# Recurrence of a bidirectional RWKV-7 layer: merged products on TensorE, one sum on GpSimd, wider state copies

## The reference, cut to what matters

```python
def _rwkv7_step(S, inp):
    r, w, k, v, a, b = inp
    Sa = jnp.einsum('zbhvk,zbhk->zbhv', S, a)
    S = S * w[..., None, :] + Sa[..., :, None] * b[..., None, :] + v[..., :, None] * k[..., None, :]
    return S, jnp.einsum('zbhvk,zbhk->zbhv', S, r)
_, ys = lax.scan(_rwkv7_step, S0, xs)          # 256 steps, two directions
y = jnp.moveaxis(ys[:, 0] + jnp.flip(ys[:, 1], axis=0), 0, 1)
```

## Time and profile before

| what | value |
|---|---|
| median of three executions | 1836.3 us |
| the profiled execution | 1839.07 us, its span 1837.1 us |
| TensorE busy in the span | 1708.0 us (93%) |
| VectorE busy | 586.1 us (32%) |
| ScalarE busy | 353.8 us (19%) |
| GpSimd busy | 64.0 us (3%) |
| recurrence (grams of pair 0 to last outputs of pair 7) | 377.6 to 613.4 us |

### The profile page before, as it was taken

One profiled execution on the slowest core, in us unless ns is written; L12 is line 12 of the kernel. 1 busy time (PEld: TensorE's weight loads), 2 busy tenths in 40 slices (PEclk: granted clock), 3 DMA queues, 4 the chain that ended last, 5 costly groups with the idle time before them and its releaser, 6 DMA issues.

```text
span 1837.1 us, 37200 instructions
## 1 busy us (share of the span) xinstructions
PE 1708.0 (93%) x16166; PEld 1090.9 (59%) x16166; DVE 586.1 (32%) x1300; ACT 353.8 (19%) x945; POOL 64.0 (3%) x96
## 2 busy tenths in 40 slices
PE   5999999988889899999899999999999999999897
PEld 5887888867777544675555455454544454444443
DVE  2000333478886301012222322313132222222233
ACT  2122222156675201123100000000000000000002
POOL 1000000000000000002000000000000000000000
PEclk9999999999999999999899999999999999999999
DMA  9932335200000753527799999999999999999993
GB/s 274 237 110 92 118 113 180 100 3 4 4 4 4 275 184 128 177 92 288 279 424 432 426 430 429 434 426 432 431 428 432 430 429 429 433 428 431 429 421 146
DMA packets 95825, 503.64 MB, mean 274 GB/s; under 512 B 37852, under 2 KB 42352, under 8 KB 76896
## 3 DMA queue, kind: packets, MB, share of 16 engines
q1 hardware_dynamic: 90824, 488.17, 66.4%
q0 software_dynamic: 4640, 13.10, 2.4%
q10 hardware_dynamic: 248, 0.65, 0.1%
HBM read 511.29 MB, written 4.23 MB: 281 GB/s over the span
## 4 chain that ended last, share of the span: by engine, by line
PE 71%; DMA 20%; DVE 6%; issue 2%; ACT 1%; SPq 0%; DVEq 0%; POOLq 0%; ACTq 0%
PE ps L1518 14%; DMA ring<-in_wd 9%; PE ps L2027 9%; DMA rest<-in_wu 8%; PE ps L2149 8%; PE ps L2016 8%; PE ps L1843 6%; PE ps L2035 4%; DMA ring<-in_wu 2%; PE ps L1861 2%; PE ps L1912 2%; PE ps L1929 2%; PE ps L1870 2%; PE ps L2007 1%; PE ps L1732 1%
## 5 line engine op out<-in xcount | busy, mean ns | idle before, releaser
L1518 PE MATMUL ps<-wide,ring 128*128 128x256 f32 x1248 | 275.3, 379 | 3.1 <-ACT wide L539 1.9
L1518 PEld LDWEIGHTS ps<-wide,ring 128*128 128x128 f32 x1248 | 239.0, 195 | 41.8 <-issue 10.1
L1397 DVE TENSOR_TENSOR tokA<-tokA,ps 128x512 f32<-128x512 f32 x256 | 158.4, 680 | 100.3 <-PE ps L2035 100.3
L2027 PE MATMUL ps<-ring,wide 128*64 128x256 f32 x1512 | 169.5, 382 | 17.1 <-DMA ring<-in_wu 17.1
L2149 PE MATMUL ps<-ring,gg 128*64 128x512 f32 x768 | 175.4, 598 | 2.7 <-DMA ring<-in_wd 2.1
L2016 PE MATMUL ps<-ring,wide 128*64 128x256 f32 x1536 | 173.2, 383 | 2.4 <-DVE wide L1385 1.7
L1410 DVE SCALAR_TENSOR_TENSOR gg<-ps,tmp,gg 128x256 f32<-128x256 f32 x32 | 15.5, 484 | 477.6 <-PE ps L2027 477.6
L2027 PEld LDWEIGHTS ps<-ring,wide 128*64 128x64 f32 x1512 | 109.6, 138 | 74.7 <-DMA ring<-in_wu 22.1
L2016 PEld LDWEIGHTS ps<-ring,wide 128*64 128x64 f32 x1536 | 110.0, 138 | 56.7 <-issue 3.3
L2035 PE MATMUL ps<-wide,gg 64*128 64x512 f32 x512 | 135.3, 627 | 0.9 <-ACT wide L815 0.8
L2149 PEld LDWEIGHTS ps<-ring,gg 128*64 128x64 f32 x768 | 50.9, 136 | 121.1 <-issue 111.1
(11 more groups left out here) (365 smaller groups left out, 2047.8 us busy)
## 6 DMA issues: line engine op xcount, KB each, us to landing
ring<-in_wg SPq DMA_DIRECT2D x23, 4096.0 KB, 28.4
ring<-in_wu SPq DMA_DIRECT2D x23, 4096.0 KB, 31.3
ring<-in_wd SPq DMA_DIRECT2D x22, 4096.0 KB, 32.1
rest<-in_wd SPq DMA_DIRECT2D x8, 4096.0 KB, 30.4
ring<-in_w_in SPq DMA_DIRECT2D x7, 4096.0 KB, 15.3
rest<-in_wu SPq DMA_DIRECT2D x7, 4096.0 KB, 30.6
rest<-in_wg SPq DMA_DIRECT2D x7, 4096.0 KB, 29.7
ring<-in_w_out SPq DMA_DIRECT2D x4, 4096.0 KB, 17.1
```

What stands on the lines that cost most here:

```text
L1397: V.tensor_tensor(fin_part(t, h, n), fin_part(t, h, n), ps[:, banks[q][h], :], ALU.add).then_inc(S["added"], 1)
L1518: ins = mm(ps[0:rows_, m % 2, 0:T], lhs, hnT[:, k, :], start=k == 0, stop=k == KD - 1)
L2027: ins = mm(ps[CAP * h:CAP * h + CAP, 1, 0:T], xT[:, k, CAP * i:CAP * i + CAP], w[:, T * h:T * h + T], start=k == 0, stop=k == KD - 1)
```

## The change

Four edits, all inside one pair of the recurrence.

First, in step 5 the two products of chunk c with the same weights (one against GB, one against NB) become one product with 128 moving columns, read as two blocks of 64 (`two_blocks`), whose result goes to two blocks of one PSUM bank. For each g there are then two products of 64 columns and two of 128. The readout correction now lies in columns 0 to 63 and the transition in 128 to 191, and VectorE reads them there.

Second, in step 6 GpSimd first adds the key grams of both directions, two instructions for each pair (tile KS), and TensorE multiplies the values with the sum: 12 products for each b in place of 16. They wait for a new semaphore rw_ks.

Third, in `inputs` both heads are taken at once: weights of 64 rows by 128 columns, 128 moving columns, two products for each (i, z) in place of four. The result is 128 by 128, of which the two diagonal 64x64 blocks are used. Tile SS is widened to take it.

Fourth, ScalarE copies 128 columns of the state (line 687) in place of 64.

Together that is 8 + 8 + 12 = 28 products fewer for each pair.

```diff
--- before.py
+++ after.py
@@ -185,7 +185,8 @@
         KT = late[:, 1536:2048].rearrange("p (z t) -> p z t", z=2)
         BKh = late[:, 2048:3072].rearrange("p (m z t) -> p m z t", m=2, z=2)
         NB = late[:, 3072:4608].rearrange("p (g n) -> p g n", g=4)
-        SS = late[:, 5120:5376].rearrange("p (z i n) -> p z i n", z=2, i=2)
+        KS = late[:, 5632:5888].rearrange("p (b e n) -> p b e n", b=2, e=2)
+        SS = late[:, 5120:5632].rearrange("p (z i n) -> p z i n", z=2, i=2)
         RH = late[:, 7680:8192].rearrange("p (g t) -> p g t", g=4)
         nrm_ = tmp[:, 0:5 * T].rearrange("p (i t) -> p i t", t=T)
         Yp, DEV, VAR, DSQ, BNS = (nrm_[:, i] for i in range(5))
@@ -262,7 +263,7 @@
         sq_done var_done std_done rw_nrm rw_vare rw_std hn_done hn_tr hn_ev_a hn_ev_v tile_mm tile_ev tile_sh lora_act
         lora_mm lora_ev v_tr v_ev rel_mm rel_ok sc_mm sc_sum sc_max pr_done pt_tr pt_ev o_mm ya_done ya_sq ya_hn
         ya_tr ya_ev rw_sq rw_n2 rw_bonus_in rw_bon rw_q rw_exp rw_prep rw_n2e rw_y0e rw_gram rw_mask rw_gnow rw_v0 rw_sums rw_pv rw_kv rw_x0
-        rw_x0ev rw_pt rw_pte rw_rh rw_tte rw_r1 rw_xf rw_xe rw_y0 rw_s rw_se rw_ys rw_yp
+        rw_x0ev rw_pt rw_pte rw_rh rw_tte rw_r1 rw_xf rw_xe rw_ks rw_y0 rw_s rw_se rw_ys rw_yp
         rw_mu rw_dsq rw_var rw_out op_mm op_add xk_mm xk_ev xs_mm xs_max xs_exp xs_p xs_tr xs_trev xo_mm xo_ev
         xw_mm xw_add r_wr r_rows r_tr r_ev r_evv r_mm r_m r_pos r_posok r_oh r_ohv r_tab r_tabok r_cnt r_cntv
         m_gate m_sil m_up m_hg m_tr m_xe m_htr m_hT m_dn m_ya m_yv r_oht r_ohtok r_vals r_pick fin_a comb added w_part gate_rest fin_o pool_step""".split()
@@ -462,6 +463,9 @@
             for n in range(4 * CT):
                 pool.wait_ge(S["rw_mask"], n + 1)
                 pool.tensor_tensor(PRN[1][:, n % 4, :, 1, :], GB[:, n % 4, :, 0, :], eye, ALU.add).then_inc(S["rw_r1"], 1)
+                if n % 4 == 3:
+                    for b in range(TB):
+                        pool.tensor_tensor(KS[:, b], GK[:, b, :, 1, :], GK[:, 2 + b, :, 1, :], ALU.add).then_inc(S["rw_ks"], 1)
             pool.wait_ge(S["rw_tte"], 4 * CT)
             pool.dma_start(tokA[:], a["x"].rearrange("(b p) d -> p b d", p=P)).then_inc(S["x2_in"], 16)
             pool.dma_start(memtok, a["mem"].rearrange("(b p) d -> p b d", p=P)).then_inc(S["mem_in"], 16)
@@ -684,7 +688,7 @@
                 for i in range(3):
                     for z in range(2):
                         act.wait_ge(S["rw_s"], 6 * p + 2 * i + z + 1)
-                        A(SS[:, z, i % 2, :], ps[:, S_BANK[i % 2] + 2 * z, T:T + CH], ACT.Copy).then_inc(S["rw_se"], 1)
+                        A(SS[:, z, i % 2, :], ps[:, S_BANK[i % 2] + 2 * z, T:T + P], ACT.Copy).then_inc(S["rw_se"], 1)
                 if next_:
                     for n in range(3, 8):
                         exponential(p + 2, n)
@@ -1135,10 +1139,10 @@
                     if g == 3 and not last:
                         bonus(p + 1, ps[:, 5, T:2 * T])
                     rh = RH[:, g, :].rearrange("p (c t) -> p c t", c=2)
-                    dc.add(V.tensor_tensor(rh, rh, ps[:, 2 * g:2 * g + 2, P:P + CH], ALU.add))
+                    dc.add(V.tensor_tensor(rh, rh, ps[:, 2 * g:2 * g + 2, 0:CH], ALU.add))
                     c = 1 - b
                     V.scalar_tensor_tensor(TT[:, g, :], cst[:, IC:IC + CH], gam_now[:, 4 * z + 1 + b:4 * z + 2 + b],
-                                           ps[:, 2 * g + c, 0:CH], ALU.mult, ALU.add).then_inc(S["rw_tte"], 1)
+                                           ps[:, 2 * g + c, P:P + CH], ALU.mult, ALU.add).then_inc(S["rw_tte"], 1)
                 if not last:
                     dve.wait_ge(S["rw_tte"], 4 * p + 4)
                     V.tensor_copy(gam_now, gam).then_inc(S["rw_gnow"], 1)
@@ -1680,6 +1684,10 @@
                 def value(q, b, e):
                     return Vtok[q, b, P * p + CH * e:P * p + CH * e + CH]
 
+                def two_blocks(x, y):
+                    assert x.ap[0] == y.ap[0] and y.offset > x.offset
+                    return bass.AP(tensor=x.tensor, offset=x.offset, ap=[x.ap[0], [y.offset - x.offset, 2], [1, CH]])
+
                 def tiles():
                     return [(e, r, half_of(r), half_of(r ^ e)) for e in range(2) for r in range(2)]
 
@@ -1747,14 +1755,15 @@
                 for g in range(4):
                     c = 1 - g % 2
                     pe.wait_ge(S["rw_xe"], 4 * p + g + 1)
-                    for h in range(2):
+                    for h in (1 - c, c):
                         q = half_of(h)
                         for e in range(2):
-                            mm(ps[half_of(e), 2 * g + h, P:P + CH], X[q, g, 1, e, :], GB[q, g, e, 1, :], start=True, stop=True)
-                    q = half_of(c)
-                    for e in range(2):
-                        ins = mm(ps[half_of(e), 2 * g + c, 0:CH], X[q, g, 1, e, :], NB[q, g, P + CH * e:P + CH * e + CH],
-                                 start=True, stop=True)
+                            if h != c:
+                                mm(ps[half_of(e), 2 * g + h, 0:CH], X[q, g, 1, e, :], GB[q, g, e, 1, :], start=True, stop=True)
+                            else:
+                                both = ps[half_of(e), 2 * g + h, 0:T].rearrange("p (k n) -> p k n", k=2)[:, :, 0:CH]
+                                ins = mm(both, X[q, g, 1, e, :], two_blocks(GB[q, g, e, 1, :], NB[q, g, P + CH * e:P + CH * e + CH]),
+                                         start=True, stop=True)
                     if g == 2 and not last:
                         pe.wait_ge(S["rw_bonus_in"], p + 2)
                         ins = mm(ps[:, 5, T:2 * T], ones2, ew[:, BON], start=True, stop=True)
@@ -1767,10 +1776,11 @@
                             q = half_of(h)
                             for e in range(2):
                                 mm(ps[half_of(e), 2 * b + h, T:T + CH], X[q, g, 0, e, :], GB[q, g, e, 1, :], start=z == 0, stop=False)
-                        for h in range(2):
-                            q = half_of(h)
-                            for e in range(2):
-                                ins = mm(ps[half_of(e), 2 * b + h, T:T + CH], value(q, b, e), GK[q, g, e, 1, :], start=False, stop=z == 1)
+                    pe.wait_ge(S["rw_ks"], 2 * p + b + 1)
+                    for h in range(2):
+                        q = half_of(h)
+                        for e in range(2):
+                            ins = mm(ps[half_of(e), 2 * b + h, T:T + CH], value(q, b, e), KS[q, b, e, :], start=False, stop=True)
                     ins.then_inc(S["rw_y0"], 1)
                 pe.wait_ge(S["rw_tte"], 4 * p + 4)
 
@@ -1782,12 +1792,9 @@
                     for z in range(2):
                         c, g, h = chunk(i, z)
                         q = half_of(h)
-                        for e in range(2):
-                            mm(ps[half_of(e), S_BANK[i % 2] + 2 * z, T:T + CH], NB[q, g, P + CH * e:P + CH * e + CH], X[q, g, 0, e, :],
-                               start=True, stop=False)
-                        for e in range(2):
-                            ins = mm(ps[half_of(e), S_BANK[i % 2] + 2 * z, T:T + CH], NB[q, g, T + CH * e:T + CH * e + CH], value(q, g % 2, e),
-                                     start=False, stop=i == 0)
+                        heads = ps[:, S_BANK[i % 2] + 2 * z, T:T + P]
+                        mm(heads, NB[q, g, P:T], X[q, g, 0].rearrange("p e n -> p (e n)"), start=True, stop=False)
+                        ins = mm(heads, NB[q, g, T:T + P], Vtok[q, g % 2, P * p:P * p + P], start=False, stop=i == 0)
                         if i == 0:
                             ins.then_inc(S["rw_s"], 1)
                     if i:
@@ -1797,14 +1804,15 @@
                     c, g, h = chunk(i, z)
                     for e in range(2):
                         q = half_of(e)
-                        ins = mm(ps[q, S_BANK[i % 2] + 2 * z, T:T + CH], TT[q, g, :], SS[q, z, (i - 1) % 2, :], start=False, stop=True)
+                        n = slice(CH * e, CH * e + CH)
+                        ins = mm(ps[q, S_BANK[i % 2] + 2 * z, T + CH * e:T + CH * e + CH], TT[q, g, :], SS[q, z, (i - 1) % 2, n], start=False, stop=True)
                     ins.then_inc(S["rw_s"], 1)
 
                 def outputs(i, z):
                     c, g, h = chunk(i + 1, z)
                     for e in range(2):
                         q = half_of(e)
-                        ins = mm(ps[q, 5 + 2 * z, T + CH * c:T + CH * c + CH], SS[q, z, i % 2, :], RH[q, g, CH * h:CH * h + CH],
+                        ins = mm(ps[q, 5 + 2 * z, T + CH * c:T + CH * c + CH], SS[q, z, i % 2, CH * e:CH * e + CH], RH[q, g, CH * h:CH * h + CH],
                                  start=True, stop=True)
                     ins.then_inc(S["rw_ys"], 1)
```

## The result

The changed kernel takes 1861.99 us (median of four executions, 1861.01 to 1863.51) against 1837.01 (1834.95 to 1843.52) for the kernel before: a ratio of 1.0132, interval 1.0119 to 1.0145. The forecast was 1839.5 with a range of 1833.5 to 1844: the sign is right, the size is not. The profiled execution has a span of 1859.2 us, 22.1 more than the 1837.1 of before; the medians are 25.0 apart.

What follows compares the result with a forecast made beforehand. TensorE bounds middle pairs from the states to turn 7, VectorE from there to the fourth transition. 7 x 0.64 = 4.5 us more, less 0.1, 0.6 and 0.6, gives +3.2: 1836.3 + 3.2 = 1839.5 us, range 1833.5 to 1844.

Steps and rivals of the forecast that it cites:

- the last of the sum: Behind the recurrence: everything waits for rw_yp of the last pair, so the recurrence's +3.2 us passes on whole.
- The block rate is the path: Rival, whole recurrence: instruction supply bounds it, so fewer instructions give 7 us, 1829; with a per-matmul overhead variant, chance 0.14.
- GpSimd slows VectorE: Rival, y0's key-gram additions: they delay VectorE 0.3 us a pair where no reserve is, 1841.6 us; chance 0.12.
- the reserve: VectorE's waits at L1065 in the recurrence, taken as 1.7 us for each pair, enough to absorb GpSimd's additions.
- GpSimd loses, not VectorE: Beside the added key-gram sums: GpSimd's operation slows from 0.41 to 0.52 us beside a VectorE copy; cost taken as 0.
- Row halves do not overlap: Rival, state inputs: each inputs call costs 0.44 us more, two on the path, 7 us in all, 1846.5; chance 0.1.
- the tail is covered: Rival, end of each pair: tile changes, loads and copies hide, a pair loses 0.2 us, not 0.64; 1836.5, chance 0.14.
- inputs(1): State-input products of both heads, on the path in each pair: 0.69 us, 0.21 more than before.
- the tail: End of each pair, inputs and last state copies: 0.21 + 0.32 + 0.11 = 0.64 us more.
- drain on a change of tiling mode: At inputs(2), going from 64x64 to 64x128 tiles drains TensorE; without that rule a pair would lose 0.10 us less.
- VectorE's time plus the 0.6: Pair 2: its third standstill moves within the readout, comes 0.5 us earlier, and the pair falls to VectorE's time, 0.6 less.
- The one at 607.62: Pair 7: this instruction standstill in the readout falls behind it, early in y0, which waits for its block until about 607.8.

Runs made afterwards that it cites:

- experiment 4: The changed kernel with its state inputs on 64x64 tiles with 128 moving columns, twice the products, no tile change: 1839.78 us, ratio 1.0009 to the kernel before.
- experiment 3: Parts of the change on the kernel before: edits 1 and 2 1836.54 us, edit 1 1836.99, edit 2 1837.25; edits 3 and 4 plus 16 padding instructions 1839.74.
- experiment 1: The kernel before with 32 small products (128 instructions) added ahead of the router's last stage, recurrence untouched: 1864.38 us, ratio 1.0135.
- experiment 5, the kernel with 128: The kernel before with 32 small products (128 instructions) round the four quarters, behind the recurrence's last outputs: 1857.25 us, ratio 1.0101.

## Why the prediction was wrong, step by step

**The step that failed** is the last of the sum: "What comes behind waits for rw_yp of the last pair, the loads of the output projection too, so it passes on whole." It treats the program behind the recurrence as untouched, because its text is. I had worked out the 256-instruction blocks, and had counted how the 112 instructions of each pair shift their bounds through the recurrence; I stopped the count at its end. Carried on to the loop it gives the shift of half a block, and the question whether the loop still stays resident. The page had the hint: TensorE issues some 23,420 instructions up to the first branch back, 92 blocks, five more passes of the loop are 31 more and the experts behind it 6; with 97 packets in all, the loop was being kept, and a thing that is kept can be lost. The term left out is 21.3 us from the first branch back to the end of the experts; the experiments show that the place of the loop makes it, while the race inside it is argued. The step failed in the small too: of the 4.4 us of the recurrence 3.6 are given back ahead of the loop, some 2.4 where the granted clock is higher and 1.0 by a shorter wait for a DMA.

**Which way the rivals fell.** None of the four was it. "The block rate is the path" looked at the right resource at the wrong place: in the recurrence the blocks come in 3.5 to 3.8 us with the DMA engines nearly idle (share 0.02 to 0.14), and cost little. "GpSimd slows VectorE" was right in its mechanism, 0.25 us a pair, and wrong in where it counts: it lies in the reserve. My reading that "GpSimd loses, not VectorE" was wrong. So was the size of the reserve: (17.1 - 6.8) / 6 = 1.7 us averages in a wait of 4.75 us in pair 6; in pairs 1 to 5 VectorE waits 1.1 us each at L1065, still enough. "Row halves do not overlap" and "the tail is covered" are excluded by 0.72 us for inputs(1) and 0.63 for the tail.

**What held.** Edit 3 and 4: inputs(1) 0.72 us (0.69), tail +0.63 (0.64), copies 276 ns (277), middle pairs of 29.5 (29.5). The Trainium skill's drain on a change of tiling mode (TensorEngine Tiling, Key Properties), weighed at 0.10 us a pair in the forecast, has 0.17 us of the tail for it in experiment 4, as far as the two kernels differ there by that alone; the pairs as a whole do not show it. Edits 1 and 2 at nothing in the middle pairs: experiment 3 says the same, pairs of 28.9. Pair 2 fell to VectorE's time plus the 0.6, as forecast, and the last standstill of pair 7 (611.47 in the earlier trace rows) is gone. The one at 607.62 fell early into y0, as forecast: it is at 612.85 now, 0.69 us ahead of L1778. The two ahead of it, in the weight loads of pair 7 after:

```profile
605.35 0.14 PEld L1735 LDWEIGHTS ps<-ring 64*64 64x64 f32 x4 [1.29 <-issue]
...
609.10 0.15 PEld L1743 LDWEIGHTS ps<-ring,cst_sb 64*64 64x64 f32 x4 [1.70 <-issue]
```

**What was mis-sized.** The recurrence by 1.2 us. Pair 0 fits (33.96 from 33.39, +0.57, forecast 0.54), and so do pairs 2 to 5. Pair 1 took 29.79, 0.25 above the forecast; pair 6 grew from 28.41 to 29.68, 1.27 in place of 0.64; pair 7, to the end of its sums, went from 29.7 to 29.4, a gain of 0.3 in place of 0.6. These three sum to 1.2. I took pair 6 for a middle pair, although the prediction says that the bounds were followed through all others. The trace shows what was missed: a bound falls into its readout. TensorE stands 1.0 us until 582.88 there, 0.7 us after ScalarE's last copy has ended, and VectorE then waits 0.25 us for the bonus product (L1769, at 584.11); before, the bound of that pair fell into y0, and VectorE waited for no product of the readout there. Ahead of inputs(0) pair 6 takes 25.88 us in place of 25.24, and 25.24 in the kernel with edits 3 and 4 alone, so its extra 0.64 is not edit 3's. For pairs 1 and 7 that is likely but was not followed up. Over the kernels without edit 3, pair 6 takes 28.4 to 29.2, and pair 0 from 32.0 to 33.9, the kernel before with padding behind it included: a microsecond of the recurrence cannot be charged to one edit from one profile each.

## What to carry to other kernels

Before instructions are added to or taken from a long unrolled program, count the blocks (256 instructions here) that each loop behind them touches, and where in a block it starts: a loop just short of what the engine keeps can be lost by a change far ahead of it, and four idle products can win it back. When a kernel loses far more than the changed stage shows, compare the counts of instruction packets and the "issue" rows first; and pad in both directions before an edit is judged by its total time.

## What the runs showed of the hardware beyond what was expected

- TensorE keeps a loop of 1,602 instructions resident when it touches seven blocks of 256; at eight it fetches nine blocks in every pass when it reaches 42 or 58 instructions into the last, and in two of five passes at 26.
- Refetching costs up to 12.7 us of standstill at the top of a pass (experiment 1). The first blocks come 6 to 7.5 us apart there (packets at 1112.5, 1118.5 and 1126.0 in the kernel after), with the DMA engines 95% busy with expert weights; with a DMA share of 0.12 they came in 3.75. A lone such pass cost 2.4 us, five in a row 5.5 each.
- Small products on one quarter of the array are serial at 0.108 us a pass, at a granted clock of 0.50 (1.2 GHz). Going round the four quarters at a clock of 1.00, 60 passes took 1.05 us (experiment 5, the kernel with 128).
- Two GpSimd additions of 128x128 (0.91 us) beside two VectorE operations of 128x256 slowed these from 0.74 to 0.99 us.
